# Layer norms split per token tile, with matmuls on the first tile placed beside the second tile's norm

## What is computed

```
h = layer_norm(x)
for l in range(DEPTH):                       # DEPTH = 2
    ada = (c_act @ w_ada[l] + b_ada[l])[:, None, :]
    sh1, sc1, g1, sh2, sc2, g2 = jnp.split(ada, 6, axis=-1)
    u = h * (1.0 + sc1) + sh1
    y = mixer(u, w_in[l], ..., w_out[l], slopes)
    h = layer_norm(DN_ALPHA * h + g1 * y, ln1_g[l], ln1_b[l])
    u = h * (1.0 + sc2) + sh2
    y = swiglu(u, w1[l], w3[l], w2[l])       # (silu(u @ w1) * (u @ w3)) @ w2
    h = layer_norm(DN_ALPHA * h + g2 * y, ln2_g[l], ln2_b[l])
```

## Time and profile before

| | us |
|---|---|
| median of 3 runs | 2552.78 |
| lowest, highest | 2552.23, 2553.62 |
| the profiled execution | 2552.34 |
| its span, first to last instruction | 2550.5 |
| PE busy in the span | 2427.4 (95%) |
| DVE busy | 876.3 (34%) |
| ACT busy | 466.0 (18%) |

### The profile page before, as it was taken

The page is one execution under the profiler, slowest core; times in us unless marked ns, Lnnn a source line. Parts: engine busy times, 40 slices in busy tenths (PEclk is TensorE's granted clock), DMA queues, the critical chain, the costliest instruction groups (busy, mean ns, idle before and its releaser), DMA issues.

```text
span 2550.5 us, 22774 instructions
## 1 busy us (share of the span) xinstructions
PE 2427.4 (95%) x9282; PEld 1613.8 (63%) x9282; DVE 876.3 (34%) x1891; ACT 466.0 (18%) x944; POOL 69.3 (3%) x101
## 2 busy tenths in 40 slices
PE   6999998999999999989999998999999989978998
PEld 4888685886478867868846454544444454547843
DVE  4663312221336532133372666720000035533001
ACT  1222310000011323000012453212100032421100
POOL 1000000000000000000010000000000001000000
PEclk9999999999999999999999999999999999989999
DMA  9753333575475333446683003442212226023441
GB/s 392 283 199 132 116 134 130 184 259 212 157 263 198 132 128 121 149 156 237 225 310 120 34 34 139 167 142 89 74 66 93 72 91 254 27 105 135 164 141 66
DMA packets 163319, 390.90 MB, mean 153 GB/s; under 512 B 6288, under 2 KB 10768, under 8 KB 160400
## 3 DMA queue, kind: packets, MB, share of 16 engines
q1 hardware_dynamic: 134400, 276.61, 30.5%
q0 software_dynamic: 26256, 102.12, 10.8%
q10 hardware_dynamic: 2560, 10.72, 1.1%
HBM read 388.37 MB, written 1.05 MB: 153 GB/s over the span
## 4 chain that ended last, share of the span: by engine, by line
PE 67%; DVE 3%; ACT 2%; issue 1%; DVEq 0%; ACTq 0%
PE bank L455 65%; ACT arena L1131 1%; PE bank L453 1%; DVE arena L1647 1%; DVE arena L1653 1%; DVE arena L1650 1%; ACT arena L1134 1%; ACT L1131 0%; DVE arena L1716 0%; DVE arena L2219 0%; DVE arena L1752 0%; DVE arena L2251 0%; DVE arena L2256 0%; DVE arena L1857 0%; DVEq L2095 0%
## 5 line engine op out<-in xcount | busy, mean ns | idle before, releaser
L455 PE MATMUL bank<-arena 128*128 128x256 f32 (+5 forms) x8794 | 2366.4, 439 | 57.0 <-DVE arena L1650 31.7
L455 PEld LDWEIGHTS bank<-arena 128*128 128x128 f32 (+2 forms) x8794 | 1552.5, 190 | 858.3 <-issue 670.7
L1653 DVE SCALAR_TENSOR_TENSOR arena<-arena 128x1028 f32<-128x1028 f32 (+5 forms) x410 | 360.1, 892 | 454.8 <-ACT arena L1131 356.1
L1647 DVE TENSOR_TENSOR arena<-bank,arena 128x512 f32<-128x512 f32 (+3 forms) x115 | 78.5, 691 | 625.1 <-PE bank L455 623.6
L1134 ACT ACTIVATE arena<-bank 128x512 f32<-128x512 f32 x227 | 127.4, 596 | 757.1 <-PE bank L455 709.5
L1131 ACT ACTIVATE arena<-arena 128x512 f32<-128x512 f32 (+7 forms) x291 | 155.3, 554 | 453.8 <-DVE arena L1727 181.7
L1647 DVE TENSOR_TENSOR arena<-arena 128x256 f32<-128x256 f32 (+7 forms) x230 | 94.1, 427 | 325.6 <-DMA arena<-in_post 271.5
L1131 ACT ACTIVATE arena<-bank 128x512 f32<-128x512 f32 (+1 forms) x135 | 65.9, 504 | 751.8 <-PE bank L455 751.0
L2352 POOL DMA_DIRECT2D arena<-in_w_ada x88 | 62.8, 713 | 2241.4 <-DVEq L1662 2235.3
L453 PE MATMUL bank<-arena 128*128 128x128 f32 x488 | 69.0, 296 | 56.7 <-DVE arena L1650 38.6
L1653 DVE SCALAR_TENSOR_TENSOR arena<-bank,arena 128x254 f32<-128x254 f32 (+3 forms) x208 | 96.2, 501 | 51.7 <-PE bank L453 35.8
(11 more groups left out here) (28 smaller groups left out, 103.9 us busy)
## 6 DMA issues: line engine op xcount, KB each, us to landing
arena<-in_w_ada POOLq DMA_DIRECT2D x96, 1028.0 KB, 6.6
arena<-in_w_in SPq DMA_DIRECT2D x84, 1024.0 KB, 7.3
arena<-in_w SPq DMA_DIRECT2D x60, 1024.0 KB, 7.4
arena<-in_w_mlp_in SPq DMA_DIRECT2D x32, 1024.0 KB, 7.5
arena<-in_w_mlp_out SPq DMA_DIRECT2D x32, 1024.0 KB, 6.7
arena<-in_w_gla SPq DMA_DIRECT2D x12, 1024.0 KB, 7.3
arena<-in_w_a SPq DMA_DIRECT2D x8, 1024.0 KB, 7.0
arena<-in_w_out SPq DMA_DIRECT2D x8, 1024.0 KB, 6.2
```

Source lines behind the costliest of these rows:

```text
L455: ins = nc.tensor.matmul(out, lhsT, rhs, start=start, stop=stop)
L1647: return V.tensor_tensor(out, x, y, op)
L1653: return V.scalar_tensor_tensor(out=out, in0=x, scalar=s, in1=y, op0=op0, op1=op1, **kw)
```

## The change

It adds `normalise_tile`, `tile_modulated` and `tile_transposes`, which do one token tile, and `half_tiles`, which does `W1 0` and `W3 0` for one token tile with 128-column matmuls. The square roots become one per tile (`root_of`, there already). The layer-to-layer `settled` waits are replaced by waits for the steps that are needed. `columns` moves ahead of the residual instructions in both places. At the layer boundary PE does the `VM` matmuls of token tile 0 for k = 0 to 3 between the two tiles' transposes; their two banks are held out of the ring meanwhile.

```diff
+            def tile_transposes(tag, tt):
+                for h in range(2):
+                    key = f"{tag} {tt} {h}"
+                    ps = open_tile(key)
+                    for e in range(4):
+                        ft = 4 * h + e
+                        mm(ps[:, e * P:e * P + P], H[:, tt, ft * P:ft * P + P], ident, t=True, done=key if e == 3 else None)
+            def half_tiles(keys, ws, n, tt, tiles):
+                for key, w in zip(keys, ws):
+                    if tt == 0:
+                        tiles[key] = open_tile(key)
+                    ps = tiles[key]
+                    for j in range(2):
+                        for i in range(KD):
+                            if i % 4 == 0 and j == 0:
+                                drained(f"U {tt} {i // 4}")
+                            mm(ps[:, j * T + tt * P:j * T + tt * P + P], w[i][:, (2 * n + j) * P:(2 * n + j + 1) * P],
+                               UT[:, i, tt * P:tt * P + P], start=(i == 0), stop=(i == KD - 1),
+                               done=key if tt and j == 1 and i == KD - 1 else None)
...
# PE, layer boundary
-                    settled(pe, f"layer {l - 1}")
+                    pe.wait_ge(dve_of[f"layer {l - 1}"], DV.of(f"layer {l - 1}", "ln2 0"))
+                    tile_transposes("T", 0)
...
+                    for k in range(4):
+                        wides[k] = wide()
+                        if k == 0:
+                            drained("T 0 0")
+                        for n in (0, 2):
+                            values_of(k, n)
+                    pe.wait_ge(dve_of[f"layer {l - 1}"], DV.of(f"layer {l - 1}", "ln2 1"))
+                    tile_transposes("T", 1)
...
+                    if l and k % 4 == 0:
+                        drained(f"T 1 {k // 4}")
+                        drained(f"T 0 {k // 4}")
...
+                        if l == 0 or k >= 4 or n % 2:
+                            values_of(k, n)
...
# PE, after WO
-                pe.wait_ge(dve_done, DV.at("ln1"))
-                transposes("U")
-                for i in range(4):
-                    drained(f"U {i}")
-                j = 0
-                for p in range(6):
+                pe.wait_ge(dve_done, DV.at("ln1 0"))
+                tile_transposes("U", 0)
+                w1, w3, tiles = panel(), panel(), {}
+                half_tiles(("W1 0", "W3 0"), (w1, w3), 0, 0, tiles)
+                pe.wait_ge(dve_done, DV.at("ln1 1"))
+                tile_transposes("U", 1)
+                half_tiles(("W1 0", "W3 0"), (w1, w3), 0, 1, tiles)
+                feature_tiles("W1 1", w1, 1, UT)
+                feature_tiles("W3 1", w3, 1, UT)
+                release(w1 + w3)
+                j = 2
+                for p in range(1, 6):
...
# ACT
-                    act.wait_ge(dve_done, DV.at("cols T"))
-                    for i in (0, 2):
-                        modulated("T", i)
+                    act.wait_ge(dve_of[f"layer {l - 1}"], DV.of(f"layer {l - 1}", "cols T"))
+                    tile_modulated("T", 0, (0, 1))
+                    act.wait_ge(dve_of[f"layer {l - 1}"], DV.of(f"layer {l - 1}", "ln2 1"))
+                    tile_modulated("T", 1, (0,))
...
-                root("ln1")
+                root_of("ln1", 0)
                 act.wait_ge(dve_done, DV.at("cols U"))
-                for i in (0, 2):
-                    modulated("U", i)
+                tile_modulated("U", 0, (0, 1))
+                root_of("ln1", 1)
+                tile_modulated("U", 1, (0,))
...
-                    for tt in range(NT):
-                        root_of("ln2", tt)
-                else:
-                    root("ln2")
+                for tt in range(NT):
+                    root_of("ln2", tt)
...
# DVE
+            def normalise_tile(name, tt):
+                c = slice(tt, tt + 1)
+                dve.wait_ge(dve_done, DV.count)
+                V.bn_aggr(mv[:, tt, :], stats[:, 12 * tt:12 * tt + 12]).then_inc(dve_done, DV.step(f"{name} moments {tt}"))
...
+                ts(H[:, tt, :], H[:, tt, :], mv[:, tt, 0:1], rstd[:, c], ALU.subtract, ALU.mult).then_inc(
+                    dve_done, DV.step(f"{name} {tt}"))
...
+                columns("U", 3)
                 for half in range(2):
                     for tt in range(NT):
                         residual(f"WO {half} {tt}", tt, half, 0)
-                normalise("ln1")
-                columns("U", 3)
-                dve.wait_ge(dve_done, DV.count)
-                for i in (1, 3):
-                    modulated("U", i)
+                        if half:
+                            normalise_tile("ln1", tt)
+                tile_modulated("U", 1, (1,))
```

More of the change, by code:

```diff
@@ L568, in _, with values_of @@
                 if l:
-                    settled(pe, f"layer {l - 1}")
+                    pe.wait_ge(dve_of[f"layer {l - 1}"], DV.of(f"layer {l - 1}", "ln2 0"))
+                    tile_transposes("T", 0)
+                o_keys, v_keys = [f"O {i}" for i in range(4)], [f"VM {i}" for i in range(4)]
+                tiles, wides = {}, {}
+                def values_of(k, n):
+                    if k == 0:
+                        tiles[v_keys[n]] = open_tile(v_keys[n])
+                        st["held"].add(marks[Progress.phase, "bank", v_keys[n]])
+                    tt = n % 2
+                    mm(tiles[v_keys[n]][:, :], UT[:, k, tt * P:tt * P + P], wides[k][:, PW * (n // 2):PW * (n // 2) + PW],
+                       start=(k == 0), stop=(k == KD - 1), done=v_keys[n] if k == KD - 1 else None)
                 if l == 0:
                     pe.wait_ge(dve_done, DV.at("x"))
-                transposes("T")
-                o_keys, v_keys = [f"O {i}" for i in range(4)], [f"VM {i}" for i in range(4)]
-                tiles = []
-                for k in range(KD):
[L576 to L579, removed]
+                    transposes("T")
+                else:
+                    for k in range(4):
+                        wides[k] = wide()
+                        if k == 0:
+                            drained("T 0 0")
[3 more added lines that the diff above has]
+                    tile_transposes("T", 1)
+                for k in range(KD):
+                    if k not in wides:
+                        wides[k] = wide()
+                    if l and k % 4 == 0:
+                        drained(f"T 1 {k // 4}")
+                        drained(f"T 0 {k // 4}")
+                    elif l == 0 and k == 0:
+                        drained("T 0")
+                    elif l == 0 and k % 2 == 0:
                         pe.wait_ge(dve_done, DV.at(f"mod {k // 2}"))
@@ L1173, in root_of, with tile_modulated @@
                 func(rstd[:, tt:tt + 1], mv[:, tt, 1:2], ACT.Sqrt, bias=LN_EPS).then_inc(act_done, AC.step(f"{name} root {tt}"))
+            def tile_modulated(tag, tt, hs):
+                for h in hs:
+                    act.wait_ge(pe_done, PE.at(f"{tag} {tt} {h} full"))
+                    ps = tile(f"{tag} {tt} {h}")
+                    for e in range(4):
+                        ft = 4 * h + e
+                        func(UT[:, ft, tt * P:tt * P + P], ps[:, e * P:e * P + P], ACT.Identity, scale=colA[:, ft:ft + 1],
+                            bias=colB[:, ft:ft + 1]).then_inc(act_done, AC.drained(f"{tag} {tt} {h}" if e == 3 else None))
             def root(name):
@@ L1699, in affine @@
             def affine(tag):
-                dve.wait_ge(pe_done, PE.at(f"{tag} 3 full"))
+                dve.wait_ge(pe_done, PE.at(f"{tag} 1 1 full"))
                 for tt in range(NT):
@@ L1722, in reciprocal_root, with tile_modulated @@
                 stt(r, t, 1.5, r, ALU.add, ALU.mult).then_inc(dve_done, DV.step())
+            def normalise_tile(name, tt):
+                c = slice(tt, tt + 1)
+                dve.wait_ge(dve_done, DV.count)
+                V.bn_aggr(mv[:, tt, :], stats[:, 12 * tt:12 * tt + 12]).then_inc(dve_done, DV.step(f"{name} moments {tt}"))
+                dve.wait_ge(dve_done, DV.count)
+                ts(var[:, c], mv[:, tt, 1:2], LN_EPS, None, ALU.add).then_inc(dve_done, DV.step())
+                dve.wait_ge(act_done, AC.at(f"{name} root {tt}"))
+                dve.wait_ge(dve_done, DV.count)
+                reciprocal_root(rstd[:, c], rstd[:, c], var[:, c], newton[:, c])
+                dve.wait_ge(dve_done, DV.count)
+                ts(H[:, tt, :], H[:, tt, :], mv[:, tt, 0:1], rstd[:, c], ALU.subtract, ALU.mult).then_inc(
+                    dve_done, DV.step(f"{name} {tt}"))
+            def tile_modulated(tag, tt, hs):
+                for h in hs:
+                    dve.wait_ge(pe_done, PE.at(f"{tag} {tt} {h} full"))
+                    ps = tile(f"{tag} {tt} {h}")
+                    for e in range(4):
+                        ft = 4 * h + e
+                        ts(UT[:, ft, tt * P:tt * P + P], ps[:, e * P:e * P + P], colA[:, ft:ft + 1], colB[:, ft:ft + 1],
```

(7 more changed lines are left out.)

20 lines of the change are left out of this document (5 added, 15 removed).

## The result

| | before | changed |
|---|---|---|
| median of 4 runs, us | 2553.20 | 2537.07 |
| lowest to highest | 2552.23 to 2553.82 | 2534.69 to 2539.02 |
| the profiled execution | 2552.34 | 2537.61 |
| its span | 2550.5 | 2535.8 |

The ratio is 0.9938, with a 95% interval of 0.9926 to 0.9951: 16.1 us faster. The prediction had the direction and the mechanism, but a gain of 11.3; its range ended at 2538.3, above the measured median.

What follows compares the result with a forecast made beforehand. TensorE, busy 95% of the span, was taken as the bound. Savings of 5.1 + 5.1 at the ln1 seams and 1.1 at ln2, 11.3 us off 2552.34, gave 2541.0, as a median 2541.5; range 2538.3 to 2547.0.

Steps and rivals of the forecast that it cites:

- the saving of 5.1 us at each ln1: At ln1 of both layers: the first pair is full 20.6 us after PE stops instead of 25.7.
- step 2: At ln1: PE transposes tile 0 at full clock in 0.91 us, then idles 1.56 for ACT's drain.
- step 3: At ln1: after four matmuls PE waits 0.48 us for ACT to drain U 0 1.
- step 4: At ln1's half pairs: a 128-column record costs 0.119 us; the first half pair has 64 of them.
- step 6: At ln1: tile 1's transposes take 0.91 us, the drain wait 1.56, then 64 records 7.6.
- Nothing waits: At ln1: affine and ACT's parameter DMA issues come some 3.5 us later, without making anything wait.
- ln2: At ln2 of layer 0: PE idles 3.5 and 1.56 us, the clock falls behind the first, 1.1 us saved.
- the rival of the held clock: At ln2: the clock doesn't fall in the pause, 1.65 us more saved, 2539.8; chance 22%.
- It falls at ln1 too: At ln1: the clock falls there as well, 1.65 us per seam, 2544.8, or 2548.1 with longer stretches; chance 20%.
- Weight loads: In the half pairs: 128-column matmuls are bound by weight loads, 190 ns a record, 2559.7; chance 4%.
- Given back: Later in the stage: a resource other than PE sets its end and the saving waits there, 2552.8; chance 7%.

Runs made afterwards that it cites:

- e7: Changed kernel, but at ln1 no matmuls between the two tiles' transposes and W1 0 and W3 0 in 256 columns again: 2549.75 us, ratio 0.9984.
- e1: The changed kernel run again with no edit: 2537.52 us, ratio 0.9940.
- e3: The kernel before with the change at the layer boundary (ln2) alone, both ln1 seams as before: 2551.30 us, ratio 0.9988.
- e8: The kernel before run again with no edit, for its trace: 2554.35 us in one run.
- e4: Changed kernel with ACT's square root of ln2's tile 1 moved behind the drains of T 0 0 and T 0 1: 2532.60 us, ratio 0.9923.
- e5: Changed kernel with PE waiting per 128x128 drain instead of per bank of four, half pairs going feature tile by feature tile: 2529.29 us, ratio 0.9902.
- e6: Changed kernel with both the late square root at ln2 and the waits per feature tile: 2527.36 us, ratio 0.9894.
- e10: The kernel of e6 run again beside e9: 2526.83 us, ratio 0.9892.
- e9: The kernel of e6 with half of the 16-column matmuls moved behind QK 0: 2524.76 us, ratio 0.9885.

## Why the prediction was wrong

**The step that failed: the saving of 5.1 us at each ln1.** The mechanism was right and this term was too small. In the traces it measured 6.48 in layer 0 and 6.58 in layer 1, because steps 2, 3, 4 and 6 took 20.65 us for what took 19.39, and because PE could go on 0.15 sooner than its row ends. With the seams as measured (6.48, 6.58 and 1.4) the forecast would have been 2538.3, just the lower end of the range; the other 1.6 of the 16.1 lies outside the terms of the sum.

**The views and the bound: right.** PE was the bound, the seams were its pauses, and what shortened them came through in full up to the last norm. Nothing was given back, and no DMA or DVE stage took over. "Nothing waits" was not quite so: DVE waits 3.36 for ACT at the first product of W3, without cost to PE. e7 shows the mechanism as told: dense work hides the norm.

**Terms of ln1: too large a cost, by 1.4 in layer 0.** Piece by piece, from the start of the transposes:

| | predicted | measured |
|---|---|---|
| to the first matmul (step 2) | 0.91 + 1.56 = 2.47 | 2.35 |
| first half pairs with the wait for U 0 1 (steps 3, 4) | 8.09 | 7.66 |
| second transposes and wait (step 6) | 2.47 | 2.20 |
| second half pairs (steps 4, 6) | 7.62 | 7.18 |
| sum | 20.65 | 19.39 |

- *Step 4, the price of a record.* 56 records take 452.29 - 445.94 = 6.35, so 0.113, and the last 64 take 7.18, 0.112 (the second product of W3 at 475.81, less 0.27, less 13.87, is 461.67). I had 0.119, because the row of 12.26 runs to the modelled end of its last matmul, some 0.15 behind the place where the next could start. 120 records at 0.006 are about 0.8 us. So the split itself cost 0.6 us, not 1.4.
- *Steps 2, 3 and 6, the wait for a drain.* The 0.31 from a drain to PE was read at a drain by DVE. ACT's fourth piece ends, by an even share of its row, at 442.98 + 2.91 / 2 = 444.43 and PE starts at 444.63, 0.20 later.
- *The stop of PE.* The same modelled end: WO's row of 27.73 ends at 441.24, but in the changed kernel the transposes start 27.58 after WO began (442.28 - 414.70). 0.15 per seam.
- 1.26 + 0.15 = 1.4, and 5.07 + 1.4 is the 6.48 measured. In layer 1 the same stretch, to the second product of W3, went from 67.68 to 61.10, 6.58. The other 0.22 of the 6.80 is one later pair of W1 and W3 that took 14.09 instead of 13.87 in the trace of before. Such a pair, up to 0.8 longer, stands in e1, e3 and e8 too and not in the changed kernel's first trace, so it comes with the execution; its cause is open.

**ln2: right in kind, 0.3 low.** The order of ACT's stream did make a pause of 3.3, the clock did fall behind it (in the traces of the change, e1, e3 and e7: four of four, for 3.4 us in three and 6.8 in e3) and held at 1.27 (e4) and 2.24 (e5). In the trace the seam gave 1.4, which is 3.12 less the 1.7 of the fall at 751.7; e3 had 2.0 by its median and 0.3 in its trace, against 1.1.

**The sum.** With 6.48, 6.58 and 1.4 the sum is 14.5, and 14.7 with the odd pair, instead of 11.3. That is also the difference of the two profiled executions. In these two traces the falls of the clock in the 16-column stage nearly cancel, together with the -0.51 behind the last norm. In layer 0 a fall of 3.4 us costs 1.2: WO starts at 413.3 to 413.7 in the five traces without any fall before it and at 414.6 to 414.7 in the three with this one alone (the -1.19 of the balance). In layer 1 it costs 1.7: from the second transposes at ln2 to the next ones, in the same code, it is 144.76 in e3, with the fall, and 143.08 in the changed kernel, without. The other 1.4 of the 16.1 is between these executions and the medians: before's lies 0.9 above, the changed kernel's 0.5 below. Only profiled executions show where the clock fell, so its cause stays open. If layer 1's fall belongs to the kernel before, as the traces so far allow, it would be part of the gain and of about this size.

**The range.** I gave it 1.5 below the rival of the held clock, and took three runs within 1.4 us for the spread of an execution. In batches of 15 runs the kernel before goes from 2548.3 to 2557.9. The trace of before also had a half-clock stretch away from the seams, at 751.7, and the sum has no term for it.

**The rivals.** *The clock holds at ln2*: no. *It falls at ln1 too*: no, in no trace of a kernel with dense work there. The rule of the Trainium skill (TensorE: Matmul & The Clock Gate, Part 4: PE-mode transpose), that transposes don't count as busy in the way a matmul does, stays unsettled: by it PE stands still at ln1 from 442.28 to 444.63, 2.35 us, and the clock held behind a plain wait of 3.01 as well. *Weight loads*: no, 0.113 is far from 0.163. *Given back*: no.

## What to carry to other kernels

Where a reduction per row stands between two dense stages, split it by tile and give PE matmuls on the first tile while the second is normed; splitting the norm alone was worth 0.6 us, with the matmuls 6.5. Then read the order of the helper engine's stream against the new seam: one square root in front of the drains cost 3.7 us here, and waits per bank instead of per piece some 5 more (e4 to e6). A sum from a profile should use starts of instructions, not modelled ends, and its range should hold the spread of executions.

## What the runs showed that I had not expected

- In a stage in which PE is called busy but each matmul has 16 columns the clock can fall as behind a pause: 12 falls in 22 stages, nine of 3.4 us at half rate and three of 6.8. Cutting the stage in two left none in the one trace taken. That is weak evidence, as e1 and e4 had none with the stage whole; but e5, e6 and e10, the nearest relatives of e9, all had one in layer 1.
- Float32 matmuls of 128 columns cost 0.112 to 0.113 a record, against half of 0.2167 = 0.108 for one of 256. Halving the columns was nearly free, although each record of 128 columns has its own weight load (PEld has 128 records more too).
- A pause that ends in transposes and drains at half clock makes the next dense stage start slow for longer: in e7, an earlier start by 1.3 us bought only 0.56.
